# Gate projection cut into eight parts among the attention groups, SiLU at the end, key selection inside the groups

## The reference

```python
h = split_cols(u @ w_in)                 # queries, keys, values, indexer, gate: 1024 columns
# dsa: indexer scores, the 64 best keys of each row, attention on these (4 heads)
isc = einsum("bth,bths->bts", iw, relu(einsum("bthd,bsd->bths", iq, ik)))   # causal: else -inf
_, idx = lax.top_k(isc, topk)            # topk = 64
# fox: 6 heads with a decay; nsa: 6 heads in a compressed, a windowed and a selected form
mix = concatenate([o_dsa, o_fox, o_nsa], -1)
y = (mix * silu(h["gate"])) @ w_out      # the gate is wanted only here
x = layer_norm(ALPHA * x + (1.0 + gate) * y, ln_g, ln_b)
```

## Time and profile before

| | us |
|---|---|
| three runs, median | 2393.32 |
| lowest, highest | 2391.03, 2450.62 |
| the profiled execution's own time | 2391.5 |
| its span | 2389.7 |
| PE busy | 2186.4 (91%) |
| DVE busy | 1460.6 (61%) |
| ACT busy | 984.5 (41%) |

### The profile page before, as it was taken

The page is one execution under the profiler, slowest core; times in us unless marked ns, Lnnn a source line. Parts: engine busy times, 40 slices in busy tenths (PEclk is TensorE's granted clock), DMA queues, the critical chain, the costliest instruction groups (busy, mean ns, idle before and its releaser), DMA issues.

```text
span 2389.7 us, 27225 instructions
## 1 busy us (share of the span) xinstructions
PE 2186.4 (91%) x10330; PEld 1726.4 (72%) x10330; DVE 1460.6 (61%) x1734; ACT 984.5 (41%) x1067; POOL 346.2 (14%) x234
## 2 busy tenths in 40 slices
PE   3999989999896879998778799999999999999997
PEld 3684656856584849987575687878788787878786
DVE  4224642145457533303963797878797897879786
ACT  0111511012112324431131575757666775757573
POOL 0000500000053237871720000000000000000000
PEclk9887788977897989998989899999999999999998
DMA  8253332432053026544400498989899898989894
GB/s 318 71 180 121 114 119 71 160 141 71 22 183 98 1 71 194 176 159 162 141 1 18 176 372 304 370 302 374 333 341 373 303 369 303 369 316 371 306 371 159
DMA packets 238542, 502.07 MB, mean 210 GB/s; under 512 B 11242, under 2 KB 52866, under 8 KB 238338
## 3 DMA queue, kind: packets, MB, share of 16 engines
q1 hardware_dynamic: 238466, 501.03, 58.7%
HBM read 499.96 MB, written 1.05 MB: 210 GB/s over the span
## 4 chain that ended last, share of the span: by engine, by line
PE 81%; DVE 12%; POOL 3%; ACT 2%; issue 1%; DMA 1%; SPq 0%; DVEq 0%; ACTq 0%; POOLq 0%
PE bank L1304 13%; PE bank L1289 9%; PE bank L1291 9%; PE bank L1290 9%; PE bank L700 6%; PE bank L888 5%; DVE cacc L2018 4%; PE bank L1007 3%; POOL ring_r L1686 3%; PE bank L1032 2%; PE bank L1183 2%; PE bank L839 2%; PE bank L987 2%; PE bank L707 2%; DVE qkv L2037 2%; PE bank L1213 2%
## 5 line engine op out<-in xcount | busy, mean ns | idle before, releaser
L2251 DVE TENSOR_TENSOR ring_r<-ring,more_his 128x2048 fp32r<-128x2048 f32 x192 | 433.5, 2285 | 10.6 <-ACT more_his L1334 10.4
L1334 ACT ACTIVATE more_his<-ring 128x2048 fp32r<-128x2048 f32 x192 | 359.0, 1908 | 13.5 <-DMA ring<-in_moe_w_down_dram 13.4
L1290 PE MATMUL bank<-ring_r,xe_hi 128*128 128x512 f32 x896 | 353.4, 394 | 0.0
L2251 DVE TENSOR_TENSOR ring_r<-ring,ring_r 128x2048 fp32r<-128x2048 f32 x144 | 325.2, 2286 | 24.9 <-ACT ring_r L1334 24.7
L1334 ACT ACTIVATE ring_r<-ring 128x2048 fp32r<-128x2048 f32 x144 | 268.0, 1907 | 3.8 <-DVE items L2218 3.8
L1289 PE MATMUL bank<-more_his,xe_hi 128*128 128x512 f32 x512 | 201.6, 394 | 0.0
L1291 PE MATMUL bank<-more_his,xe_lo 128*128 128x512 f32 x512 | 199.6, 390 | 0.0
L1290 PEld LDWEIGHTS bank<-ring_r,xe_hi 128*128 128x128 f32 x896 | 171.2, 191 | 34.7
L1304 PE MATMUL bank<-ring_r,he_hi 128*128 128x512 f32 x640 | 182.5, 391 | 0.0
L1289 PE MATMUL bank<-ring_r,xe_hi 128*128 128x512 f32 x384 | 156.7, 408 | 23.1 <-DVE ring_r L2251 23.1
L1686 POOL TENSOR_TENSOR ring_r<-ring,ff_hi 128x2048 fp32r<-128x2048 f32 (+1 forms) x34 | 156.9, 4640 | 91.1 <-ACT ff_hi L1334 91.1
(11 more groups left out here) (407 smaller groups left out, 3653.6 us busy)
## 6 DMA issues: line engine op xcount, KB each, us to landing
ring<-in_moe_w_gate_dram SPq DMA_DIRECT2D x112, 1024.0 KB, 5.2
ring<-in_moe_w_up_dram SPq DMA_DIRECT2D x112, 1024.0 KB, 5.3
ring<-in_moe_w_down_dram SPq DMA_DIRECT2D x112, 1024.0 KB, 4.9
ring<-in_w_in_dram SPq DMA_DIRECT2D x16, 2048.0 KB, 8.2
ring<-in_w_ada_dram SPq DMA_DIRECT2D x12, 2048.0 KB, 8.1
ring<-in_w_out_dram SPq DMA_DIRECT2D x8, 2048.0 KB, 7.8
ring<-in_w_in_dram SPq DMA_DIRECT2D x10, 1536.0 KB, 6.7
ring<-in_ffn_w_gate_dram SPq DMA_DIRECT2D x11, 1024.0 KB, 5.4
```

The costliest lines, as they stand in the source:

```text
L1290: mm(b[:, :], xe_hi[:, k, :], lo[:, kk, :], start=False, stop=False)
L1334: return go(out, in_, ACT.Copy, scale=scale)
L2251: tt(piece_lo(p), piece_raw(p), piece_hi(p).bitcast(fp32), ALU.subtract).then_inc(S("lo_ready"), 1)
```

## The change

The gate projection is no longer one block. The four banks of `gt` are each filled by two parts of four matmuls. Part 0 stays ahead of `ckv`, parts 1 to 7 stand in groups 1 to 7: an odd part after the scores, an even one after the transposes (`GT_AT`). All four use bank 6. ACT copies each bank into `sg` unchanged, in groups 2, 4, 6 and 8, and one SiLU per token tile over 1024 columns follows after the last group's exponentials; DVE waits for it by `gate_silu_done`. The selection becomes `select(step)`, 16 rounds spread over groups 1 to 14 (`SEL_FROM`, `SEL_BY`); groups 7 and 14 have two rounds, the others one. `ada_gate` moves from groups 7 and 9 to 9 and 11, its `ada_step`s over the first 10 groups instead of 7.

```diff
@@ -173,9 +173,11 @@
 GROUPS = attention_groups()
 NG = len(GROUPS)
 
-GATE_AT = {7: 0, 9: 1}
+GT_AT = {0: 0, 2: 1, 4: 2, 6: 3}
+GATE_AT = {9: 0, 11: 1}
 NEXT_AT = {14: 0, 16: 1, 18: 2, 21: 3}
-GATE_BY, NEXT_FROM, NEXT_BY = 7, 4, 16
+GATE_BY, NEXT_FROM, NEXT_BY = 10, 4, 16
+SEL_FROM, SEL_BY = 1, 15
 MIX_COL = {"dsa": 0, "fox": 256, "cmp": 640, "win": 640, "slc": 640}
 GATE_OF = {"cmp": 0, "slc": 1, "win": 2}
 
@@ -209,11 +211,10 @@
     add("nq01", 6); add("nq2", 2); add("kcvc", 3)
     add("rot_nq01", 4); add("ks", 5); add("rot_nq2", 6)
     add("vsw", 2); add("kwg", 7); add("rot_ks", 4); add("ch", 3); add("rot_kw", 5)
-    for c in range(2):
-        for i in range(NT):
-            add(f"gt{c}{i}", [6, 2][i])
     add("ckv", 3, 2)
     for k in range(NG + 2):
+        if k in GT_AT:
+            add(f"gt{GT_AT[k] // 2}{GT_AT[k] % 2}", 6)
         if k < NG:
             add(f"S{k}", [0, 1, 7][k % 3])
         if 1 <= k <= NG:
@@ -830,15 +831,20 @@
                                   start=(t == 0), stop=(t == CMP_LEN // 2 - 1))
                 done(last, j)
                 rotate(l, "kw")
-                for c in range(2):
-                    for i in range(NT):
-                        j = jobs[l, f"gt{c}{i}"]
-                        b = take(pe, j)
-                        w = weights(pe, (l, f"gate{c}"))
-                        for k in range(KD):
-                            last = mm(b[:, :], uT[:, k, i * P:(i + 1) * P], w[:, k, :], start=(k == 0), stop=(k == KD - 1))
+
+                def gate_part(n):
+
+                    r = GT_AT[n - n % 2]
+                    c, i = r // 2, r % 2
+                    j = jobs[l, f"gt{c}{i}"]
+                    b = take(pe, j)
+                    w = weights(pe, (l, f"gate{c}"))
+                    for k in range(n % 2 * (KD // 2), (n % 2 + 1) * (KD // 2)):
+                        last = mm(b[:, :], uT[:, k, i * P:(i + 1) * P], w[:, k, :], start=(k == 0), stop=(k == KD - 1))
+                    if n % 2:
                         done(last, j)
 
+                gate_part(0)
                 j = jobs[l, "ckv"]
                 b = take(pe, j)
                 pe.wait_ge(S("ch_ready"), l + 1)
@@ -958,8 +964,12 @@
                 for n in range(NG + 2):
                     if n < NG:
                         scores(n)
+                    if n % 2 and n - 1 in GT_AT:
+                        gate_part(n)
                     if 1 <= n <= NG:
                         transposes(n - 1)
+                    if n and n in GT_AT:
+                        gate_part(n)
                     if n >= 2:
                         outputs(n - 2)
                     if n in GATE_AT:
@@ -1397,16 +1407,16 @@
                 free(go(sgate[:, :, :], b[:, T:T + 36], ACT.Exp, scale=-1.0), j)
                 j = jobs[l, "ch"]
                 go(ch[:, 0, :, :], filled(act, j)[0:HD, 0:60], ACT.Exp, scale=-1.0).then_inc(S("ch_exp"), 1)
-                for c in range(2):
-                    for i in range(NT):
-                        j = jobs[l, f"gt{c}{i}"]
-                        free(go(sg[:, i, 512 * c:512 * c + 512], filled(act, j)[:, :], ACT.Silu), j)
                 j = jobs[l, "ckv"]
                 b = filled(act, j)
                 copy(kcT[0:HD, :, :], b[0:HD, 0:30])
                 free(copy(kcT[HD:P, :, :], b[0:HD, 0:30]), j)
 
                 for n, (kind, i, heads, keys) in enumerate(GROUPS):
+                    if n - 2 in GT_AT:
+                        c, r = GT_AT[n - 2] // 2, GT_AT[n - 2] % 2
+                        j = jobs[l, f"gt{c}{r}"]
+                        free(copy(sg[:, r, 512 * c:512 * c + 512], filled(act, j)[:, :]), j)
                     if l + 1 < DEPTH and NEXT_FROM <= n < NEXT_BY:
                         at, of = n - NEXT_FROM, NEXT_BY - NEXT_FROM
                         for step in range(4 * KD * at // of, 4 * KD * (at + 1) // of):
@@ -1426,6 +1436,10 @@
                         last = go(p_sb[:, n % 2, m * keys:(m + 1) * keys], b[:, m * keys:(m + 1) * keys], ACT.Exp,
                                   bias=stat[:, n % 4, 0, m:m + 1], accum_out=stat[:, n % 4, 1, m:m + 1])
                     free(last, j)
+                for r in range(NT):
+                    for c in range(2):
+                        copied(act, jobs[l, f"gt{c}{r}"])
+                    go(sg[:, r, :], sg[:, r, :], ACT.Silu).then_inc(S("gate_silu_done"), 1)
                 for i in range(NT):
                     for half in range(2):
                         j = jobs[l, f"yT{i}{half}"]
@@ -1851,17 +1865,18 @@
                 link(ts(sgate[:, :, :], sgate[:, :, :], 1.0, None, ALU.add))
                 link(nc.vector.reciprocal(sgate[:, :, :], sgate[:, :, :]))
 
-                for i in range(NT):
+                def select(step):
+
+                    i, k = step // (TOPK // 8), step % (TOPK // 8)
                     keys = (i + 1) * P
-                    link(tt(isc[:, i, keys - P:keys], isc[:, i, keys - P:keys], C("causal"), ALU.add))
-                    cur, nxt = isc, isw
-                    for k in range(TOPK // 8):
-                        link(nc.vector.max(m8[:, i, :], cur[:, i, 0:keys]))
-                        link(nc.vector.match_replace(nxt[:, i, 0:keys], m8[:, i, :], cur[:, i, 0:keys], TAKEN))
-                        cur, nxt = nxt, cur
-
-                    link(ts(isw[:, i, 0:keys], cur[:, i, 0:keys], TAKEN / 2, NEG, ALU.is_gt, ALU.mult))
-                    tt(isw[:, i, keys - P:keys], isw[:, i, keys - P:keys], C("causal"), ALU.add).then_inc(S("sel_ready"), 1)
+                    cur, nxt = (isc, isw) if k % 2 == 0 else (isw, isc)
+                    if k == 0:
+                        link(tt(isc[:, i, keys - P:keys], isc[:, i, keys - P:keys], C("causal"), ALU.add))
+                    link(nc.vector.max(m8[:, i, :], cur[:, i, 0:keys]))
+                    link(nc.vector.match_replace(nxt[:, i, 0:keys], m8[:, i, :], cur[:, i, 0:keys], TAKEN))
+                    if k == TOPK // 8 - 1:
+                        link(ts(isw[:, i, 0:keys], nxt[:, i, 0:keys], TAKEN / 2, NEG, ALU.is_gt, ALU.mult))
+                        tt(isw[:, i, keys - P:keys], isw[:, i, keys - P:keys], C("causal"), ALU.add).then_inc(S("sel_ready"), 1)
 
                 j = jobs[l, "ckv"]
                 b = filled(dve, j)
@@ -1943,15 +1958,17 @@
                     if n < GATE_BY:
                         for step in range(2 * KD * n // GATE_BY, 2 * KD * (n + 1) // GATE_BY):
                             ada_step(l, 4 + step // KD, step % KD)
+                    if SEL_FROM <= n < SEL_BY:
+                        at, of, rounds = n - SEL_FROM, SEL_BY - SEL_FROM, NT * TOPK // 8
+                        for step in range(rounds * at // of, rounds * (at + 1) // of):
+                            select(step)
                     if n in GATE_AT:
                         gate(GATE_AT[n])
                     if l + 1 < DEPTH and n in NEXT_AT:
                         shift_scale(l + 1, NEXT_AT[n])
 
-                for c in range(2):
-                    for i in range(NT):
-                        copied(dve, jobs[l, f"gt{c}{i}"])
-                for i in range(NT):
+                for i in range(NT):
+                    dve.wait_ge(S("gate_silu_done"), NT * l + i + 1)
                     tt(mix[:, i, :], mix[:, i, :], sg[:, i, :], ALU.mult).then_inc(S("mix_ready"), 1)
 
                 for c in range(2):
```

## The result

| | before | changed |
|---|---|---|
| median, us | 2394.36 (4 runs, 2391.03 to 2450.62) | 2418.46 (4 runs, 2413.37 to 2421.91) |
| ratio to before | | 1.0104, 95% interval 1.0076 to 1.0131 |
| profiled execution, us | 2391.5 | 2413.4 |
| its span, us | 2389.7 | 2411.6 |
| PE busy, us | 2186.4 | 2205.2 |

The change costs 24 us, and the forecast was 2415. The time is within the 2% that was called no change, and the interval shows a small loss. The page's line of the granted clock already says where the loss is: in the attention layers, the first 11 of 40 slices (60.3 us each), the clock is at 7 tenths or less in slices 5, 6, 10 and 11, where the earlier trace rows had slices 4, 5, 9 and 10.

A forecast was written before the change was run, and what follows sets the result against it. TensorE was taken to bound the kernel, at half clock in many attention groups. P, Q, R and S summed to +12.5 us in layer 0 and +11.0 in layer 1: 2391.5 + 23.5 = 2415 us, range 2360 to 2430 (forecast's own 2405 to 2422).

The forecast's parts named there:

- P: Projection to first score: with one gate part of eight left there, 24.1 us less in each layer.
- Q: Groups 0 to 7: seven gate parts added, mostly at full clock; +7.1 us in layer 0, +6.3 in layer 1.
- R: Groups 8 to 10: VectorE falls behind and TensorE stalls; +1 us in layer 0, +3 in layer 1.
- S: Group 11 to the mix's first transpose: half clock to the groups' end; +28.5 us in layer 0, +25.8 in layer 1.
- A: Rival: the second ada_gate pair lifts the clock again in one layer, saving about 24 us: 2391 us; chance 0.18.
- B: Rival: stalls split into small waits and both layers keep the full clock: 2364 us; chance 0.20.
- C: Rival: gate parts among the groups don't lift the clock and run at half, 41 us more a layer: 2497 us; chance 0.04.
- D: Rival: the clock falls earlier, in group 8 or the compressed groups, 5 to 12 us more a layer: 2425 to 2440; chance 0.08.

The follow-up runs named there:

- selection early: Changed kernel with the 16 selection rounds in groups 0 to 6 instead of 1 to 14, ada_steps still over 10 groups: 2385.8 us.
- both early: Changed kernel with selection in groups 0 to 6 and ada_steps over the first 8 groups, 2354.2 us, or the first 5, 2352.0 us.
- steps in 7 groups: Changed kernel with the 16 ada_steps over the first 7 groups instead of 10: 2400.9 us.
- 8 maxima: Version with selection in groups 0 to 6 and steps in 5 groups, plus 8 unread VectorE maxima in group 9 of each layer: 2414.8 us.
- short GpSimd additions: Version with selection in groups 0 to 6 and steps over 10 groups, GpSimd's additions cut to 8 of 512 columns: 2357.6 us.
- part 0 split: Version with selection in groups 0 to 6 and steps in 5 groups, half of the first gate part moved behind ckv: 2342.2 us.
- 4 maxima: Version with selection in groups 0 to 6 and steps in 5 groups, plus 4 unread VectorE maxima in group 9: 2382.3 us.

## Why the prediction was right, point by point

**P was right** to 0.3 us in each layer, and with it the claim that the selection, no longer ahead of `vblk`, leaves the first score where `ckv` puts it: 1.58 us of wait, as 1.55 before.

**Q was right**, 0.5 to 0.7 us low. In layer 0 the parts in the groups took 3.6 to 3.7 us, except for parts 1 and 4 (5.86 and 4.96 us). The record had two spells at half clock with 5 us of cost; they were 10.2 us (181.6 to 191.8) and 3.4 us (212.3 to 215.7) long, which at 0.45 of their length is 6.1 us.

**R was right in its sum and partly wrong in its place.** The record had the stall "most of it before transpose 10", with groups 8 to 10 at full clock up to there. Layer 1 is close to that: VectorE shows no wait from 555.79 us on, and TensorE waits 0.67 us before transpose 8 and 0.96 us before transpose 9, 1.6 us for the 3 forecast. In layer 0 the whole wait, 2.27 us, stood before transpose 8. The rows of DVE behind group 7 say why:

```profile
239.27 1.50 DVE L1785 SCALAR_TENSOR_TENSOR ring<-ring,vecs 128x512 f32<-128x512 f32 x1
...
242.23 1.08 DVE L1878 TENSOR_SCALAR isw<-isc 128x128 f32<-128x128 f32 x1
...
243.56 0.55 DVE L1902 TENSOR_REDUCE stat<-bank 128x3 f32<-128x384 f32 x1
```

The step takes 1.50 us here, and the closing operation L1878 of tile 0's selection, which falls into the same group as the double round, 1.08 us. In layer 1 the step is 0.75 us (557.34) and the same operation

```profile
559.56 0.23 DVE L1878 TENSOR_SCALAR isw<-isc 128x128 f32<-128x128 f32 x1
```

These two excesses, 0.75 and 0.85 us, are the 1.6 us between the waits of 2.27 and 0.67 us before transpose 8. I had priced the `ada_step`s beside GpSimd (1.0 us more) and not the selection's own operations, and had summed over groups 8 to 10 as if TensorE could spend its lead anywhere; but the row maximum of group 8 (243.56) already came too late. That the sum of R in layer 0 came out at +0.2 for +1 is luck. The waits were 2.27 + 0.26 = 2.5 us (the second before transpose 9), for 7 in the record, and the half clock from 246.4 to 254.4 cost 0.45 x 8.0 = 3.6 us that the record did not have. The Trainium skill, "SBUF — State Buffer", section "SBUF: two separate sides", has VectorE and GpSimd take turns at a port pair for whole instructions, for operations of VectorE with two SBUF inputs or in a mode with two ports; the rows agree, as L1785 and L1878 grow by 0.7 to 0.9 us there while the maxima L1875 stay at 0.29 us.

**S was right in its mechanism, with its size in layer 1 low by 2.6 us.** The record has 0.83 on 31.3 us, 25.8 (its factor unrounded is 1.15 / 0.63 - 1 = 0.825); the rows give 63.87 - 35.5 = 28.4. Two terms were left out. Scores 11 were taken as done at full clock. They start at 568.67, behind the fall, with 1.22 us a pair, and 1.9 x 0.83 = 1.6 us belong to S. The second `ada_gate` pair, which the change moves from group 9 (in R) to group 11 (in S), was not priced: 2.02 us (574.62). Against these 3.6 us stand the wait of 0.6 us near the end of the groups, which is gone at half clock, and a factor of 1.82 for the whole stretch, a little lower than 1.83. Layer 0 has the same two omissions, and its +29.3 for +28.5 is close only because the clock was up again from 318.1 us on, 4.3 us ahead of the mix, and the factor came out lower. That a short wait in the later groups brings the fall was shown by the versions: the fall goes with the wait (selection early, both early), it moves with the wait (steps in 7 groups), and it comes back with the wait (8 maxima, all four executions). It is not the only way: with short GpSimd additions, and in group 0 with part 0 split, the clock fell without a wait.

**The rivals.** A was wrong: both second L859 pairs (260.36, 574.62) took 2.02 us and the clock stayed. It had rested on layer 0 of the kernel before, where the rise stood behind the second pair; in layer 1 it stood behind the first (562.73, the rise at 565.2), so the pair alone was never a sure sign. B did not occur, but the versions with both pieces early are B, at 2352 to 2354 us. Its 2364 was too high: it added 3 us for a slower VectorE and kept the waits in R's forecast, and of these only 0.42 us before transpose 8 is left in the profiled execution with the steps in 8 groups. C was wrong, with 3.6 to 3.7 us for most parts and 5.9 for the longest. D, a fall in the groups ahead of 11, is what happened in layer 0. It cost none of D's 5 to 12 us more, since the wait was 2.3 us and not 7 and groups 9 and 10 at half clock take what they took before the change.

By the rule of the Trainium skill ("TensorE: Matmul & The Clock Gate", Part 1), which stood behind B, a busy TensorE keeps its clock. The rows speak against busy time as the measure for such matmuls: 71.34 of 71.60 us busy at 0.50 here, 42.00 of 42.00 us busy at 1.00 with the selection early, in layer 1 behind the last gate part.

**Costed at nothing, and rightly:** SiLU ends at 319.70 us, with the 1.28 us of its table load ahead of it, and so before the product that needs it (timeline of ACT, then of DVE):

```profile
317.70 2.00 ACT L1442 ACTIVATE sg<-sg 128x1024 f32<-128x1024 f32 x2
```

```profile
321.11 2.35 DVE L1972 TENSOR_TENSOR mix<-mix,sg 128x1024 f32<-128x1024 f32 x2
```

The wait before L987 is 1.46 us, for 1.59 in the earlier trace rows. The later load of `ada2` cost nothing either: ScalarE begins to scale it in group 10, at 251.96 us, right behind the exponentials of group 9 and with no idle time ahead.

## What to carry to other kernels

Where the engine that sets the end has a clock that can be lost, a wait is priced by what follows it: 3.66 us of added VectorE work in one group cost 32 us in one layer and 26 in the other, and two lines of numbers (`GATE_BY`, and `SEL_FROM` with `SEL_BY`) turned a loss of 1.0% into a gain of 2.1% (1.2 to 3.1). When work is moved in between groups, sum the helper engine's time group by group against TensorE's, with the operations that GpSimd slows down at their slowed price, and put the extra work where the dense matmuls give it cover. When an expected gain is missing, look at the granted clock in windows cut at its changes before looking for a wait of that size: here the largest new wait among the groups was 2.27 us, and S lost 57.7.

## What the runs showed of the hardware that I had not expected

- The groups behind the last gate part kept 1.00 for 46.4 us with PE busy for 44.63 us (layer 1, both pieces early), and nearly the same groups kept 0.50 for 71.6 us with 71.34 busy (layer 0, changed kernel). The later groups, 7 to 19, mostly stay at the level at which they find the clock, until something disturbs it. The first scores do not: with part 0 split they pulled it down at 182.9 us with no wait.
- A burst of 8 records of 128x512 lifted it in both layers. Two records (`ada_gate`) stood before the rise in the kernel before (the second pair of layer 0, 271.7 us; the first of layer 1, 565.2 us), and not in the changed one.
- The same program can fall in some executions and hold in others: with 4 maxima, 2351 to 2353 us four times and 2382 to 2388 us six times. A clock can also fall in the later groups with no wait in front of it (266.34 us, PE 47.70 of 47.70 us busy).
